# Where ScalarE's first partial-sum copy stands beside a weight cast in three slots of a Strassen projection

## The chip, the cores and the metric

The kernel runs on one core of one Trainium2 chip. The metric is the device time of one execution in microseconds (us). TensorE (PE) multiplies, VectorE (DVE), ScalarE (ACT) and GpSimd (POOL) do the elementwise work, SyncE (SP) issues nearly all loads.

## The reference, cut to what matters

One layer on 512 tokens of width 1024, in float32: an FFN, a mixer, a second FFN, each behind an RMS norm with shift and scale. The two FFNs are the same computation with other weights:

```python
def swiglu(h, w_in, w_out):          # w_in 1024 x 5632, w_out 2816 x 1024
    gu = h @ w_in
    g, u = jnp.split(gu, 2, axis=-1)
    return (jax.nn.silu(g) * u) @ w_out

x = x + HALF_STEP * mod[:, 0, 2][:, None, :] * swiglu(h, ffn1_w_in[l], ffn1_w_out[l])
```

## The kernel before, in words

Each float32 product is made of three passes: an operand is split into a rounded part (`_hi`) and a remainder (`_lo`), and TensorE adds hi x hi, hi x lo and lo x hi. For a weight, ScalarE casts `sw_raw` to `sw_hi` and VectorE subtracts to get `sw_lo_a` or `sw_lo_b`.

The first product of an FFN has 22 tiles of 128 gate and 128 up columns. The first 8 (FFN `f` = 0) or 2 (`f` = 1) are done plainly with 512 moving columns. The other 14 or 20 are Strassen slots `strassen(f, n)`: the tile's product, cut in half three ways, is formed from 7 half-size products ("half-products" 0 to 6) on sums of weight blocks and of activation blocks. A half-product is 12 matmuls of 256 moving columns, so a slot is 84 matmuls. Slots come in two groups, and each is followed by eight down projections (`down2`, 33 matmuls of 512 columns each) that consume 11 tiles of the hidden layer. For `f` = 0 the groups are slots 0 to 2 and 3 to 13, for `f` = 1 they are 0 to 8 and 9 to 19: `N0` = (3, 9) is the first slot of the second group.

The weights of a slot are 7 blocks in three pieces: blocks 0 and 1, blocks 2 to 4, blocks 5 and 6 (1024, 1536 and 1024 columns). Piece 0 and piece 1 are usually cast in the slot before, piece 2 in the slot itself, by `cast_up(f, n, 2)`. In a slot that follows a down projection (n = `N0[f]`) the last block of piece 1 (512 columns) is also cast in the slot, by `cast_up(f, n, 1)`. This block is added up by an accumulating DMA from POOL's queue (line 632), for which the cast waits. In all other slots after the first of an FFN the product of the slot before is finished in between.

Half-products 0, 2 and 4 accumulate in one PSUM region of which intermediate sums are needed. So ScalarE copies that region out after half-product 0 (`keep_sum(f, n, 0)`, 256 columns) before half-product 2 may add to it, half-product 1 after `keep_five` before half-product 3 is started, and so on. Each engine has its own instruction stream, written out by hand in this order; semaphores join them. TensorE's waits in a slot are, in its order: piece 0's remainder, then half-products 0 and 1; then piece 1's remainder (early part) and `q_kept` for the first copy, then half-product 2; then `q_kept` for `keep_five`, then half-product 3; after that half-products 4 to 6, with piece 2's remainder needed by half-product 5.

VectorE's stream in a slot is: remainder of piece 1, second half of the product of the slot before (chained slots), remainder of piece 2, the three weight-block sums of the next slot (`add_blocks`), remainder of its piece 0, then `late_up` and `gates`. SyncE may load the weights of slot n + 2 into a buffer once the remainders of slot n are done, and POOL issues its accumulating DMA once they have landed.

Of the kernel before, what the change touches and what calls it, by code (L numbers as in the profile page):

```python
# [36 lines left out]
def build_program(nc, x, c, w_ada, b_ada, norm_ffn1_g, ffn1_w_in, ffn1_w_out, norm_mix_g, w_mix_in,  # L37
# [62 lines left out]
    N0 = tuple(GF - p for p in PLAIN)  # L100
# [3 lines left out]
    def up_item(f, n):  # L104
        return n + (KD if n >= N0[f] else 0)
# [6 lines left out]
    def pieces(f, i):  # L112
        return sum(3 if j in UP_ITEMS[f] else 1 for j in range(i))
# [4 lines left out]
    def added(f, i):  # L118
        return 16 * sum(1 for j in range(i % 2, i + 1, 2) if j in UP_ITEMS[f])
# [34 lines left out]
    with ctx:  # L154
# [243 lines left out]
        def sw_slot(f, i):  # L398

            return sw_first[:] if f and i == 0 else sw_raw[:, i % 2]  # L400
# [276 lines left out]
        def _(act):  # L677
# [127 lines left out]
            def plain_hi(f, j):  # L805
                act.wait_ge(prod_ready, P_AT[f] + j + 1)
                nc.scalar.copy(b_hi[:, j, :], work[:, 1, :]).then_inc(a_hi_ready, 1)

            def hsum_split(f, r):
                act.wait_ge(hsum_ready[f], HSUMS[r])  # L810
                k0, cols = HSUM_AT[r]
                nc.scalar.activation(sums_hi[:, r], xs[:, k0:k0 + KA, cols], ACT.Copy,
                                     scale=-1.0 if r == 2 else 1.0).then_inc(hsum_hi[f], 1)

            def cast_up(f, n, c):

                i = up_item(f, n)
                if i == 0:
                    act.wait_ge(chunk_done, UP_AT[f] + PLAIN[f] - 1)
                elif i - 1 in UP_ITEMS[f]:  # L820
                    act.wait_ge(sw_used[f], pieces(f, i - 1) + c + 1)
                else:
                    act.wait_ge(sw_used[f], pieces(f, i) - 1 if c == 0 else pieces(f, i))
                act.wait_ge(sw_sum[f], 3 * n + c + 1)
                if c == 1:
                    act.wait_ge(sw_added[f][i % 2], added(f, i))
                j0, j1 = PIECES[c]
                if c == 1 and n == N0[f]:
                    j0 = EARLY[1]
                nc.scalar.copy(sw_hi[:, j0 * BL:j1 * BL], sw_slot(f, i)[:, j0 * BL:j1 * BL])\  # L830
                    .then_inc(sw_hi_ready[f], 1)
# [10 lines left out]
            def cast_down_early(f, g):  # L842

                i = down_item(f, g, 0)
                act.wait_ge(sw_used[f], pieces(f, i) - 2)
                act.wait_ge(sw_full[f][i % 2], landed(f, i))
                nc.scalar.copy(down_hi(0)[:, 0:EARLY_K * P], sw_raw[:, i % 2, 0:EARLY_K * P]).then_inc(early_hi[f], 1)

            def cast_down(f, g, m):

                i = down_item(f, g, m)
                act.wait_ge(sw_used[f], pieces(f, i) - 1 if m == 0 else pieces(f, i - 1))
                act.wait_ge(sw_full[f][i % 2], landed(f, i))
                c = slice(0 if m else EARLY_K * P, DN)
                nc.scalar.copy(down_hi(m)[:, c], sw_raw[:, i % 2, c]).then_inc(sw_hi_ready[f], 1)  # L855

            def keep_sum(f, n, j):

                act.wait_ge(q_done[f], 3 * n + 1 + j)
                if n:  # L860
                    act.wait_ge(gate_ready[f], n)
                nc.scalar.copy(keep[:, j], ps[:, n % 2 * 2, 0:TH]).then_inc(q_kept[f], 1)  # L862

            def keep_five(f, n):
                act.wait_ge(sw_used[f], pieces(f, up_item(f, n)) + 1)
                if n:
                    act.wait_ge(up1_ready[f], n)
                nc.scalar.copy(keep[:, 3], ps[:, n % 2 * 2 + 1, TH:T]).then_inc(q_kept[f], 1)

            def keep_third(f, n):  # L870
                act.wait_ge(sw_used[f], pieces(f, up_item(f, n)) + 2)
                nc.scalar.copy(keep[:, 2], ps[:, n % 2 * 2, 0:TH]).then_inc(q_kept[f], 1)

            def silu_both(f, n):
                act.wait_ge(gate_ready[f], n + 1)
                if n:
                    act.wait_ge(b_prod[f], 2 * n)
                nc.scalar.activation(silu_2, gate, ACT.Silu).then_inc(s_ready[f], 1)

            def product_hi(f, n):  # L880
                act.wait_ge(b_prod[f], 2 * n + 2)
                nc.scalar.copy(b_hi[:, (PLAIN[f] + n) % GF, :], work[:, 1, :]).then_inc(b_hi_ready[f], 1)

            def up_slot(f, n):
                chained = up_item(f, n) and up_item(f, n) - 1 in UP_ITEMS[f]
                second = f == 1 and n == 0
                if n and not chained:
                    cast_up(f, n, 1)
                if n:
                    cast_up(f, n, 2)  # L890
                keep_sum(f, n, 0)
                if chained:
                    product_hi(f, n - 1)
                if f == 0 and n == 0:
                    plain_hi(f, PLAIN[f] - 1)
                keep_five(f, n)
                if second:
                    hsum_split(f, 3)
                keep_sum(f, n, 1)
                if second:  # L900
                    keep_third(f, 0)
                    plain_hi(f, 1)
                if n not in (N0[f] - 1, NS[f] - 1):
                    cast_up(f, n + 1, 0)
                else:
                    cast_down_early(f, 0 if n < N0[f] else 1)
                if not second:
                    keep_third(f, n)
                if n in (N0[f] - 1, NS[f] - 1):
                    cast_down(f, 0 if n < N0[f] else 1, 0)  # L910
                else:
                    cast_up(f, n + 1, 1)
                silu_both(f, n)

            def first_group(f):
                for n in range(N0[f]):
                    up_slot(f, n)
                for m in range(KD):
                    if m < KD - 1:
                        cast_down(f, 0, m + 1)  # L920
                    else:
                        cast_up(f, N0[f], 0)
                        cast_up_early(f)
                    if m == 0:
                        product_hi(f, N0[f] - 1)
# [16 lines left out]
            for n in range(N0[0], NS[0]):  # L942
                up_slot(0, n)
# [87 lines left out]
            for n in range(N0[1], NS[1]):  # L1031
                up_slot(1, n)
# [1137 lines left out]
```

## Time and profile before

| | us |
|---|---|
| median of 3 runs | 857.15 |
| lowest and highest | 853.22 and 858.28 |
| the profiled execution | 860.13 |
| its span in the trace | 858.4 |

The span is what the instruction records cover; 1.73 us of the profiled execution lie outside. The granted TensorE clock is 0.997 of full speed over the span. TensorE is busy for 97% of the span, VectorE 75%, ScalarE 44%, POOL 6%. All times in the rows are from the start of the span of this one execution.

### The profile page before, as it was taken

The numbers are of one execution on the slowest core, as the hardware profiler recorded it, in microseconds if no ns is written. First come the engines' busy times: TensorE is split into PE (matmuls) and PEld (weight loads), VectorE is DVE, ScalarE is ACT, GpSimd is POOL, SyncE is SP. The second block draws the span as 40 slices with busy tenths as digits, with TensorE's granted clock in tenths as the row PEclk, the third lists the DMA queues.
The fourth block names the chain that finished last, engine by engine and source line by source line (L and its number), as shares of the span: only waits on it lengthen the run. The fifth ranks groups of instructions, "written<-read, shape, count | busy, mean of one in ns | idle before, by whom it ended". The sixth has DMA issues, their size and how long they took to land.

```text
span 858.4 us, 14169 instructions
## 1 busy us (share of the span) xinstructions
PE 835.3 (97%) x5767; PEld 746.7 (87%) x5767; DVE 642.7 (75%) x923; ACT 381.2 (44%) x532; POOL 48.4 (6%) x56
## 2 busy tenths in 40 slices
PE   4999999999999999999999999999999999999996
PEld 3778889888999998887887898999988899999886
DVE  4579987877888878858657779988793588885443
ACT  6233346212656652333424256666511366665323
POOL 0000000000000000000430000000000000100000
PEclk9999999999999999999999999999999999999999
DMA  9997566667666666853434802586763567663222
GB/s 282 284 316 250 147 180 207 199 199 191 168 168 166 156 196 180 251 162 100 144 93 118 219 2 74 144 189 172 208 203 106 135 156 176 160 176 107 69 68 98
DMA packets 212733, 142.02 MB, mean 165 GB/s; under 512 B 6216, under 2 KB 191676, under 8 KB 212668
## 3 DMA queue, kind: packets, MB, share of 16 engines
q1 hardware_dynamic: 207716, 132.19, 53.0%
q0 software_dynamic: 4896, 8.92, 6.9%
q8 instruction: 45, 0.74, 0.4%
q14 instruction: 20, 0.16, 0.1%
q10 hardware_dynamic: 56, 0.01, 0.0%
HBM read 130.08 MB, written 2.10 MB: 154 GB/s over the span
## 4 chain that ended last, share of the span: by engine, by line
PE 89%; DVE 4%; SPq 4%; DMA 1%; ACT 1%; issue 1%; ACTq 0%
PE ps L1702 16%; PE ps L1704 16%; PE ps L1703 15%; PE ps L1877 12%; PE ps L1879 12%; PE ps L1881 12%; SPq L485 3%; DMA ada_first<-in_w_ada_dram 1%; PE ps L2003 1%; SPq L447 1%; PE ps L2005 1%; PE ps L2004 1%; DVE h_lo L1114 1%; DVE xs L1107 1%; PE ps L1753 0%
## 5 line engine op out<-in xcount | busy, mean ns | idle before, releaser
L1877 PE MATMUL ps<-sums_hi,sw_hi 128*128 128x256 f32 x544 | 150.9, 277 | 0.6 <-ACT ev L862 0.4
L1879 PE MATMUL ps<-sums_lo,sw_hi 128*128 128x256 f32 x544 | 151.2, 278 | 0.0
L1702 PE MATMUL ps<-b_hi,sw_hi 128*128 128x512 f32 (+1 forms) x374 | 143.7, 384 | 0.0
L1703 PE MATMUL ps<-b_lo,sw_hi 128*128 128x512 f32 (+1 forms) x374 | 140.6, 376 | 0.0
L830 ACT CAST sw_hi<-sw_raw 128x1024 fp32r<-128x1024 f32 (+2 forms) x99 | 116.5, 1181 | 28.6 <-DVE sw_raw L1288 17.8
L1877 PE MATMUL ps<-h_hi,sw_hi 128*128 128x256 f32 x408 | 113.1, 277 | 0.6 <-DVE sw_lo_a L1297 0.6
L1879 PE MATMUL ps<-h_lo,sw_hi 128*128 128x256 f32 x408 | 113.3, 278 | 0.0
L1881 PE MATMUL ps<-sums_hi,sw_lo_a 128*128 128x256 f32 x408 | 112.9, 277 | 0.0
L1877 PEld LDWEIGHTS ps<-sums_hi,sw_hi 128*128 128x128 f32 x544 | 102.1, 188 | 0.9 <-DVE sw_lo_a L1297 0.6
L1879 PEld LDWEIGHTS ps<-sums_lo,sw_hi 128*128 128x128 f32 x544 | 102.0, 187 | 0.0
L1297 DVE TENSOR_TENSOR sw_lo_a<-sw_raw,sw_hi 128x1024 fp32r<-128x1024 f32 x66 | 96.0, 1455 | 5.8 <-ACT sw_hi L830 5.8
L1702 PE MATMUL ps<-h_hi,w_split 128*128 128x512 f32 (+1 forms) x224 | 86.6, 387 | 4.1 <-DVE h_lo L1114 3.9
L1703 PE MATMUL ps<-h_lo,w_split 128*128 128x512 f32 (+1 forms) x224 | 84.4, 377 | 0.0
L1704 PE MATMUL ps<-h_hi,w_split 128*128 128x512 f32 (+1 forms) x224 | 84.3, 376 | 0.0
L1703 PEld LDWEIGHTS ps<-b_lo,sw_hi 128*128 128x128 f32 x374 | 70.3, 188 | 13.5
L1702 PEld LDWEIGHTS ps<-b_hi,sw_hi 128*128 128x128 f32 x374 | 70.3, 188 | 12.3
L1877 PEld LDWEIGHTS ps<-h_hi,sw_hi 128*128 128x128 f32 x408 | 76.6, 188 | 0.9 <-issue 0.7
L1879 PEld LDWEIGHTS ps<-h_lo,sw_hi 128*128 128x128 f32 x408 | 76.5, 187 | 0.2
L1881 PEld LDWEIGHTS ps<-sums_hi,sw_lo_a 128*128 128x128 f32 x408 | 76.6, 188 | 0.0
L1881 PE MATMUL ps<-h_hi,sw_lo_a 128*128 128x256 f32 x272 | 75.3, 277 | 0.0
L855 ACT CAST sw_hi<-sw_raw 128x1408 fp32r<-128x1408 f32 (+1 forms) x32 | 40.3, 1261 | 73.9 <-PE ps L1704 67.4
L1704 PE MATMUL ps<-b_hi,sw_lo_b 128*128 128x512 f32 (+1 forms) x198 | 72.7, 367 | 0.0
(205 smaller groups left out, 1596.8 us busy)
## 6 DMA issues: line engine op xcount, KB each, us to landing
sw_raw<-in_ffn_w_in_dram SPq DMA_DIRECT2D x165, 256.0 KB, 4.4
sw_raw<-in_w_ada_dram SPq DMA_DIRECT2D x16, 1024.0 KB, 5.4
sw_raw<-in_ffn_w_out_dram SPq DMA_DIRECT2D x32, 384.0 KB, 4.4
sw_raw<-in_ffn_w_out_dram SPq DMA_DIRECT2D x32, 320.0 KB, 3.4
w_raw<-in_ffn_w_in_dram SPq DMA_DIRECT2D x19, 512.0 KB, 6.7
sw_raw<-sw_raw POOLq DMA_DIRECT2D x33, 256.0 KB, 3.4
ada_raw<-in_w_ada_dram SPq DMA_DIRECT2D x16, 512.0 KB, 6.0
ada_first<-in_w_ada_dram SPq DMA_DIRECT2D x14, 512.0 KB, 8.2
```

Source lines behind the costliest of these rows:

```text
L447: sp.dma_start(to[:, g, k0:k1], up_w(w)[:, half * KA + k0:half * KA + k1, g, 0:2 * P])\
L485: sp.dma_start(first_w(k)[:, sec], w_ada_v[:, :, col:col + P]).then_inc(first_full[k], 16)
L830: nc.scalar.copy(sw_hi[:, j0 * BL:j1 * BL], sw_slot(f, i)[:, j0 * BL:j1 * BL])\
L855: nc.scalar.copy(down_hi(m)[:, c], sw_raw[:, i % 2, c]).then_inc(sw_hi_ready[f], 1)
L1107: nc.vector.scalar_tensor_tensor(dst, src, gs[:, n, k:k + 1], r, ALU.mult, ALU.mult)\
L1297: nc.vector.tensor_tensor(lo_piece(c)[:, skip:], sw_slot(f, i)[:, j0 * BL + skip:j1 * BL], sw_hi[:, j0 * BL + skip:j1 * BL].bitcast(F32), ...
L1702: nc.tensor.matmul(dst, w_h, a_h, start=start, stop=False)
L1703: nc.tensor.matmul(dst, w_h, a_l, start=False, stop=False)
L1704: return nc.tensor.matmul(dst, w_l, a_h, start=False, stop=stop)
L1877: nc.tensor.matmul(dst, w_h[:, k, :], src_hi[:, k, :], start=start and k == 0, stop=False, skip_group_check=True)
L1879: nc.tensor.matmul(dst, w_h[:, k, :], src_lo[:, k, :], start=False, stop=False, skip_group_check=True)
L1881: ins = nc.tensor.matmul(dst, w_l[:, k, :], src_hi[:, k, :], start=False, stop=stop and k == KA - 1, skip_group_check=True)
```

## The change

In three slots, (f, n) = (0, 3), (1, 9) and (1, 1), the copy after half-product 0 is placed ahead of the cast of piece 2 in ScalarE's stream instead of behind it. No instruction, wait or increment is added or removed.

```diff
             def up_slot(f, n):
                 chained = up_item(f, n) and up_item(f, n) - 1 in UP_ITEMS[f]
                 second = f == 1 and n == 0
+                early_keep = n == N0[f] or (f, n) == (1, 1)
                 if n and not chained:
                     cast_up(f, n, 1)
+                if early_keep:
+                    keep_sum(f, n, 0)
                 if n:
                     cast_up(f, n, 2)
-                keep_sum(f, n, 0)
+                if not early_keep:
+                    keep_sum(f, n, 0)
                 if chained:
                     product_hi(f, n - 1)
```

Slots (0, 3) and (1, 9) open the second group of their FFN; slot (1, 1) is the second slot of its group, and the first with a piece 2 to cast in it.

## Rows read from the trace of the kernel before

**Rows 1.** The page's first part: TensorE's busy time, share and instructions.
```profile
PE 835.3 (97%) x5767; PEld 746.7 (87%) x5767; DVE 642.7 (75%) x923; ACT 381.2 (44%) x532; POOL 48.4 (6%) x56
```
**Rows 2.** From TensorE's waits over the span: total, times, longest (us).
```profile
PE ps L1877 <- ACT ev L862: 0.4, 1, 0.4
```
**Rows 3.** Timeline of TensorE in slot (0, 3): start, duration (us).
```profile
213.02 0.28 PE L1881 MATMUL ps<-sums_hi,sw_lo_a 128*128 128x256 f32 x1
213.43 0.36 PE L1877 MATMUL ps<-sums_hi,sw_hi 128*128 128x256 f32 x1
213.62 0.28 PE L1879 MATMUL ps<-sums_lo,sw_hi 128*128 128x256 f32 x1
```
**Rows 4.** Timeline of ScalarE there; in brackets the idle time before and its releaser.
```profile
211.44 1.58 ACT L830 CAST sw_hi<-sw_raw 128x512 fp32r<-128x512 f32 x2 [4.55 <-DMA sw_raw<-sw_raw]
212.92 0.36 ACT L862 COPY ev<-ps 128x256 f32<-128x256 f32 x1
213.33 0.37 ACT L868 COPY ev<-ps 128x256 f32<-128x256 f32 x1
```
**Rows 5.** Busy time in two windows of 100 us, matmuls into ps alone.
```profile
213.50:313.50 100.00, 100.00 (x844) 1.00 0.63 163
683.00:783.00 100.00, 100.00 (x885) 1.00 0.65 157
```
**Rows 6.** Timeline of TensorE: first matmul of each eleven-slot group, and first behind it.
```profile
210.40 0.28 PE L1877 MATMUL ps<-h_hi,sw_hi 128*128 128x256 f32 x1
...
320.21 0.40 PE L1702 MATMUL ps<-b_hi,sw_hi 128*128 128x512 f32 x1
...
680.60 0.28 PE L1877 MATMUL ps<-h_hi,sw_hi 128*128 128x256 f32 x1
...
785.33 0.39 PE L1702 MATMUL ps<-b_hi,sw_hi 128*128 128x512 f32 x1
```
**Rows 7.** Timeline of VectorE in slot (0, 3).
```profile
213.05 1.23 DVE L1297 TENSOR_TENSOR sw_lo_b<-sw_raw,sw_hi 128x1024 fp32r<-128x1024 f32 x1 [0.26 <-ACT sw_hi L830]
214.19 2.14 DVE L1288 TENSOR_TENSOR sw_raw<-sw_raw 128x512 f32<-128x512 f32 x3
```
**Rows 8.** Timelines in slots (1, 9), (1, 10); last, the page's row of POOL's DMA.
```profile
680.80 1.57 ACT L830 CAST sw_hi<-sw_raw 128x512 fp32r<-128x512 f32 x2 [4.11 <-PE ps L1704]
682.27 0.37 ACT L862 COPY ev<-ps 128x256 f32<-128x256 f32 x1
...
683.33 0.28 PE L1877 MATMUL ps<-sums_hi,sw_hi 128*128 128x256 f32 x1
...
691.01 0.87 POOL L632 DMA_DIRECT2D sw_raw<-sw_raw  x1 [12.77 <-DMA sw_raw<-in_ffn_w_in_dram]
...
697.40 1.49 ACT L830 CAST sw_hi<-sw_raw 128x1536 fp32r<-128x1536 f32 x1
...
sw_raw<-sw_raw POOLq DMA_DIRECT2D x33, 256.0 KB, 3.4
```
**Rows 9.** Timelines of VectorE and ScalarE in slot (1, 1).
```profile
543.67 1.75 DVE L1297 TENSOR_TENSOR sw_lo_a<-sw_raw,sw_hi 128x1536 fp32r<-128x1536 f32 x1
544.33 1.03 ACT L830 CAST sw_hi<-sw_raw 128x1024 fp32r<-128x1024 f32 x1
545.27 0.36 ACT L862 COPY ev<-ps 128x256 f32<-128x256 f32 x1
546.12 0.62 ACT L882 CAST b_hi<-work 128x512 fp32r<-128x512 f32 x1 [0.49 <-DVE work L1345]
546.64 0.37 ACT L868 COPY ev<-ps 128x256 f32<-128x256 f32 x1
```
**Rows 10.** Timeline of TensorE in slot (1, 1), and behind slot (1, 8).
```profile
545.77 0.36 PE L1877 MATMUL ps<-sums_hi,sw_hi 128*128 128x256 f32 x1 [0.45 <-ACT ev L862]
...
547.24 0.28 PE L1877 MATMUL ps<-h_hi,sw_hi 128*128 128x256 f32 x1
...
619.32 0.39 PE L1702 MATMUL ps<-b_hi,sw_hi 128*128 128x512 f32 x1
```

## The prediction

> **What bounds the kernel now.** I read the page's first part, then TensorE's waits, then the timeline of the three slots. TensorE is busy for 97% of the span and no other engine is near that [rows 1], so only time in which TensorE stands still, or runs slower than it could, is to be had. The list of waits puts just one wait down to the copy that the change moves, 0.4 us, once [rows 2]. By that list the change is worth 0.4 us at most. The list is not enough, though: it compares a releaser with the modelled end of the matmul before, and a stop shorter than a matmul's 0.28 us doesn't show in it. So I looked at starts.
>
> In slot (0, 3) the matmuls of half-products 0 and 1 start every 0.113 us (210.40 to 213.02 for 23 steps [rows 3, 6]). The last starts at 213.02, the next not at 213.13 but at 213.43, and the one after 0.19 later [rows 3]. ScalarE ended the copy after half-product 0 at 212.92 + 0.36 = 213.28, and 0.15 later TensorE goes on [rows 3, 4]. In slot (1, 1) the copy ends at 545.27 + 0.36 = 545.63 and TensorE goes on at 545.77, again 0.14 later [rows 9, 10]. So TensorE stood still for the copy in two of the three slots. In (1, 9) the copy was done at 682.64, and half-product 2 began on pace at 683.33 [rows 8]: no wait.
>
> **The pace behind the stop is the larger thing.** From 213.5 on, 844 matmuls start in 100 us, in the same slots of the second FFN 885 [rows 5]: 118.5 against 113.0 ns each, of the same size, with the granted clock at 1.00 in both and about the same DMA traffic (share 0.63 against 0.65). The first 24 matmuls of slot (0, 3) still have the fast pace, the slow one begins with the stop and lasts to the end of the group. The two groups are of eleven equal slots: 320.21 - 210.40 = 109.81 us against 785.33 - 680.60 = 104.73 us [rows 6]. The difference is **5.08 us**, of which the stop itself is 213.43 - 213.02 + 0.19 - 2 x 0.113 = 0.37 us and the pace 4.71 us. The stop in (1, 1), 0.45 + 0.28 - 0.11 = 0.6 us beyond the pace [rows 10], had no such sequel: from 547.24 the 48 + 7 x 84 = 636 matmuls to 619.32 took 113.3 ns each [rows 10]. So a stop can bring the slow pace, and need not; I don't know what decides it.
>
> The Trainium skill, page "TensorE: Matmul & The Clock Gate", Part 1, gives the distance of matmuls at full clock as the columns over 2.4 GHz plus a fixed 2.5 ns or so; for 256 columns that is 109 ns, one figure. The trace has two, 113.0 and 118.5 ns, both above it, at the same granted clock. By that rule only the clock changes the pace, and removing the stop would return 0.37 us and no more; this is the first rival below, whose time is worked out there from rows.
>
> **Part 1, slot (0, 3).** Nothing is added or removed, one copy and one cast change places. The cast of 512 columns started at 211.44, when the accumulating DMA had landed, and with the one of 1024 behind it took 1.58 us in all [rows 4]. The two end at 213.02; the second takes some 1.03 us, as its like in [rows 9], and so the first is over by about 212.0. Half-product 0 ends 12 matmuls before 213.02 + 0.28, at 211.94. The copy can then run from 212.0 to 212.4. Half-product 2 is due at 213.13, and with 0.15 us for the release needs it by 212.98: 0.6 us of slack, so the stop goes. What is late next? Of what half-product 2 waits for, piece 1's early remainder was made before the slot. Half-product 3, due at 213.13 + 1.36 = 214.49, needs `keep_five`; that copy waits for the end of half-product 1 at 213.30 and started at 213.33 [rows 4]. The moved cast now ends at about 213.35 instead of 213.02, so it hardly touches it. Gain: the stop, 0.37 us, and if the slow pace is its consequence, 4.71 us. Upper end 5.08; lower end 0 if another late semaphore takes the copy's place.
>
> Behind the moved cast are queued: piece 2's remainder on VectorE, 213.05 to 214.28 [rows 7], now some 0.35 later, needed by half-product 5 at 213.13 + 3 x 1.36 = 217.2, so 2.6 us of cover; and the three sums of the next slot's blocks, 214.19 to 216.33 [rows 7], now to 216.7, of which the next cast needs the first. Piece 0's remainder is then ready by about 218, and the next slot begins at 219.9: 2 us of cover. SyncE's loads for slot 5 start 0.35 us later. All cost nothing.
>
> **Part 2, slot (1, 9).** No wait to remove, so gain 0. Here the DMA was early and the 512-column cast began at 680.80 with the end of the down projections [rows 8]. ScalarE now stands idle from 681.4 to the end of half-product 0 at 682.15, copies to 682.5, and the piece 2 cast ends at 683.5 instead of 682.37: 1.1 us later. Piece 2's remainder is ready at 684.8, half-product 5 is due at 683.33 + 4.08 = 687.4. The loads of slot 11 start 1.1 us later; POOL's accumulating DMA for them was issued at 691.01 and the cast that needs it started at 697.40 [rows 8]. With 3.4 us to landing [rows 8] it is ready at 695.5 instead of 694.4, 1.9 us of cover. If that cover were gone, the price would be the difference, under 1 us. I take 0.
>
> **Part 3, slot (1, 1).** The copy moves ahead of the 1.03 us cast at 544.33 and ends at 544.7 [rows 9]. But the remainder of piece 1 ends on VectorE at 543.67 + 1.75 = 545.42 [rows 9], and half-product 2 needs it too. TensorE can start at 545.42 + 0.14 = 545.56 instead of 545.77, 0.21 earlier. Half-product 3 began at 547.24, 1.47 behind that, so it would be due at 547.03. It needs `keep_five`, at 546.64 to 547.01, which stands behind the product's cast at 546.12, which waits for VectorE's product and doesn't move [rows 9]. With the release, 547.15: 0.09 us is left of the 0.21, and a restart costs about 0.08 (the 0.19 behind a stop instead of 0.11). Gain 0.0, between -0.1 and +0.2; and this slot now has a stop of 0.4 and a new small one of 0.12 us, where before it had one of 0.6.
>
> **The sum.** Against the profiled execution: 860.13 - 5.08 - 0.0 - 0.0 = 855.05 us. The median of the runs shown lies 2.98 below the profiled execution: 852.07. The three runs lie 5.06 apart, as much as the slow pace costs; I read that, as an estimate, as the slow pace being there in 857.15 and 858.28 and absent in 853.22. The changed kernel should then be at 853.22 less up to 0.4. I take the middle of 852.07 and 852.8, **852.4 us**, its own range 850.5 to 854.2.
>
> **Rivals.**
> 1. The pace isn't the stop's doing (0.26). For: the clock is full, nothing on TensorE's waits shows it, and the stop in (1, 1) had no such sequel. Against: it begins with the matmul behind the stop, and the twin group without a stop never has it. Then 857.15 - 0.4 = 856.7. The same time comes out if the accumulating DMA lands more than 0.6 us later in most executions, so that the stop stays.
> 2. The slow pace goes from the first FFN and comes into the second (0.14), by the stops of Part 3. From half-product 3 to the end of the group are 72.1 us [rows 10]; at 118.5 instead of 113.0 ns they take 0.049 x 72.1 = 3.5 us more: 852.4 + 3.5 = 855.9. For: of the two stops, the shorter (0.30 us) was the one with the slow pace, and the new ones are short. Against: one case is no rule.
> 3. Slower than before (0.08): the same mechanism in slot (1, 1), and no cure in (0, 3), either because rival 1 holds or because the typical run before hadn't the slow pace. 857.15 + 3.5 = 860.6. It decides from the point at which `keep_five` ends later than half-product 3 is due less 0.14 us, which by the above is exceeded by 0.12 us.
> 4. The change does nothing: the copy is bound by the end of half-product 0 or the early cast anyway (0.02), 857.15. The rows speak against it in (0, 3).
>
> **Chances.** The forecast has 0.50. With 852.4 (850.5 to 854.2), 855.9 and 856.7 the range from 850.7 to 857.4 leaves out 860.6, the very ends and little else. One per cent, 8.6 us, is about what a measurement of this kernel can tell from no change; all cases but the tails lie within it: faster by over 1% 0.03, within 0.94, slower by over 1% 0.03.
>
> **What would show it.** In the profile after: matmul starts of slot (0, 3) without a step behind the 24th; the eleven slots from there in 104.7 instead of 109.8 us, 885 matmuls in 100 us; the copy of (0, 3) at 212.0 ahead of the 1024-column cast; in (1, 9) an idle ScalarE before its copy and an unchanged TensorE; in (1, 1) half-product 2 released by the remainder (line 1297) at 0.2 us earlier and half-product 3 by `keep_five`, and 113 ns to the end of that group. I am wrong if the group of (0, 3) has no stop and still 118.5 ns (rival 1), if the group of (1, 1) has 118.5 (rivals 2 and 3), or if the landing of the accumulating DMA moves about by more than 0.6 us.

## The result, and the profile after

| | before | changed |
|---|---|---|
| median of 22 executions each (us) | 854.83 | 857.78 |
| lowest and highest | 853.02, 858.68 | 852.6, 863.46 |
| executions below 855 us | 12 | 3 |
| the profiled execution, its span | 860.13, 858.4 | 856.37, 854.6 |

The ratio is 1.003, 95% interval 1.0017 to 1.0044: a small loss, where a gain of 0.6% was forecast. 857.78 lies 0.38 us above the range. The median of before itself moved with more executions, from 857.15 to 854.83. And the two profiled executions are the other way round, before 860.13, changed 856.37: one execution doesn't tell these kernels apart.

The lines of the page hardly differ. What [rows 1] showed is now:

```profile
PE 835.5 (98%) x5767; PEld 747.2 (87%) x5767; DVE 641.9 (75%) x923; ACT 381.6 (45%) x532; POOL 48.5 (6%) x56
```

The list of TensorE's waits has no row for the copy any more. Its one wait for a weight remainder, 0.6 us, is at the start of slot (1, 1) and stood in the list before too.

**Slot (0, 3)** went as forecast. The timelines of ScalarE and TensorE, answering to [rows 3, 4, 6] (lines are 4 further down than before from here on: 1881 was 1877):

```profile
209.22 0.62 ACT L830 CAST sw_hi<-sw_raw 128x512 fp32r<-128x512 f32 x1 [4.11 <-PE ps L1708]
210.59 0.37 ACT L862 COPY ev<-ps 128x256 f32<-128x256 f32 x1 [0.75 <-PE ps L1885]
210.86 1.06 ACT L830 CAST sw_hi<-sw_raw 128x1024 fp32r<-128x1024 f32 x1
```
```profile
209.02 0.28 PE L1881 MATMUL ps<-h_hi,sw_hi 128*128 128x256 f32 x1
...
211.64 0.28 PE L1885 MATMUL ps<-sums_hi,sw_lo_a 128*128 128x256 f32 x1
211.75 0.28 PE L1881 MATMUL ps<-sums_hi,sw_hi 128*128 128x256 f32 x1
...
313.75 0.39 PE L1706 MATMUL ps<-b_hi,sw_hi 128*128 128x512 f32 x1
```

The copy is over at 210.96, before half-product 2 is due; the step is 0.11 us and the eleven slots take 313.75 - 209.02 = 104.73 us instead of 109.81. But the accumulating DMA was early here: the first cast was released by TensorE and not by the DMA. By the times of [rows 8], where the DMA was early as well, the old order would have kept pace too. The case that the change was made for stands in the profile of e5, one of the experiments below, with the same new order in this slot. There the cast waited for the DMA and began 1.19 us behind the group's first matmul (209.79), against 1.04 us in before, where TensorE stopped. ScalarE and TensorE in e5:

```profile
210.98 0.62 ACT L830 CAST sw_hi<-sw_raw 128x512 fp32r<-128x512 f32 x1 [4.65 <-DMA sw_raw<-sw_raw]
211.51 0.37 ACT L862 COPY ev<-ps 128x256 f32<-128x256 f32 x1
```
```profile
212.41 0.28 PE L1885 MATMUL ps<-sums_hi,sw_lo_a 128*128 128x256 f32 x1
212.52 0.28 PE L1881 MATMUL ps<-sums_hi,sw_hi 128*128 128x256 f32 x1
```

The copy is over at 211.88, and half-product 2 starts on pace at 212.52. The profiles of e6 and e12 show the same, with casts 1.10 and 1.19 us behind the first matmul. So the new order does take this stop away.

**Slot (1, 9)** went as worked out: ScalarE stands idle for 0.75 us before its copy, the cast of piece 2 ends 2.89 us behind the group's first matmul (forecast 2.9, before 1.77), and TensorE has no step in this slot.

**Slot (1, 1)** also went as worked out, to 0.1 us. VectorE, ScalarE and TensorE, answering to [rows 9, 10]:

```profile
536.65 1.75 DVE L1301 TENSOR_TENSOR sw_lo_a<-sw_raw,sw_hi 128x1536 fp32r<-128x1536 f32 x1
```
```profile
537.31 0.35 ACT L862 COPY ev<-ps 128x256 f32<-128x256 f32 x1
537.56 1.05 ACT L830 CAST sw_hi<-sw_raw 128x1024 fp32r<-128x1024 f32 x1
539.10 0.62 ACT L882 CAST b_hi<-work 128x512 fp32r<-128x512 f32 x1 [0.49 <-DVE work L1349]
539.62 0.37 ACT L868 COPY ev<-ps 128x256 f32<-128x256 f32 x1
```
```profile
538.03 0.28 PE L1885 MATMUL ps<-sums_hi,sw_lo_a 128*128 128x256 f32 x1
538.45 0.39 PE L1881 MATMUL ps<-sums_hi,sw_hi 128*128 128x256 f32 x1
538.68 0.28 PE L1883 MATMUL ps<-sums_lo,sw_hi 128*128 128x256 f32 x1
...
539.87 0.28 PE L1885 MATMUL ps<-sums_hi,sw_lo_a 128*128 128x256 f32 x1
540.04 0.38 PE L1881 MATMUL ps<-h_hi,sw_hi 128*128 128x256 f32 x1
```

The copy ends at 537.66, the remainder at 538.40, and TensorE goes on 0.05 behind that (0.14 was forecast): the stop's step from start to start is 0.42 us instead of before's 0.72. The second stop is there too (0.17 from 539.87 to 540.04), made by `keep_five`, which ends at 539.99. In between the matmuls start every 0.119 us, the slow pace; in this execution the fast pace came back with the second stop. From its first matmul to the first one behind it, this group took 612.25 - 525.08 = 87.17 us against 87.21 before, the gain of 0.0 that was forecast.

**The slow pace is now somewhere else.** Windows, TensorE into ps alone: the eleven slots of the first FFN, then slots 9 to 11 and from 12 on of the second ([rows 5] before):

```profile
212.00:312.00 100.00, 100.00 (x885) 1.00 0.69 171
676.00:696.00 20.00, 20.00 (x179) 1.00 0.61 145
707.00:777.00 70.00, 70.00 (x593) 1.00 0.58 150
```

The bracket counts every matmul that touches a window, two or three more than start in it, so 70 us over 593 is a little low. From start to start the trace has 118.6 ns in this stretch and 113.3 ns in the first two. The slow pace begins in slot (1, 12) at a step of 0.15 us, 0.03 too long:

```profile
706.08 0.28 PE L1885 MATMUL ps<-sums_hi,sw_lo_a 128*128 128x256 f32 x1
706.23 0.39 PE L1881 MATMUL ps<-h_hi,sw_hi 128*128 128x256 f32 x1
```
```profile
701.30 1.49 ACT L830 CAST sw_hi<-sw_raw 128x1536 fp32r<-128x1536 f32 x1 [1.34 <-DMA sw_raw<-sw_raw]
...
705.28 0.62 ACT L882 CAST b_hi<-work 128x512 fp32r<-128x512 f32 x1 [0.75 <-DVE work L1349]
705.81 0.37 ACT L868 COPY ev<-ps 128x256 f32<-128x256 f32 x1
```

A cast waited 1.34 us for the accumulating DMA, what ScalarE and VectorE did behind it was late, and `keep_five` ended at 706.18, a hair too late. For 0.03 us of waiting the group took 781.72 - 673.54 = 108.18 us, 3.4 us more than the 104.73 of [rows 6].

### The profile page after: what moved, and what is told of

Same layout as the page of the kernel before. It is cut to its first block, busy times and chain, and to the rows that moved or that the text cites. A ratio compares the mean times of both kernels' runs of the same rounds, so it can differ in the third digit from the quotient of the medians.

```text
span 854.6 us, 14169 instructions
## 1 busy us (share of the span) xinstructions
PE 835.5 (98%) x5767; PEld 747.2 (87%) x5767; DVE 641.9 (75%) x923; ACT 381.6 (45%) x532; POOL 48.5 (6%) x56
## 4 chain that ended last, share of the span: by engine, by line
PE 90%; DVE 4%; SPq 3%; DMA 1%; issue 1%; ACT 1%; ACTq 0%
PE ps L1706 16%; PE ps L1708 16%; PE ps L1707 16%; PE ps L1881 12%; PE ps L1883 12%; PE ps L1885 12%; SPq L485 2%; SPq L447 1%; PE ps L2007 1%; PE ps L2008 1%; PE ps L2009 1%; DMA ada_first<-in_w_ada_dram 1%; DVE h_lo L1118 1%; DVE xs L1111 1%; DVE sw_lo_a L1301 1%
```

## The experiments

Theory S: in slot (1, 1) the changed stop brings the slow pace more often. Theory L: the later cast of piece 2 makes loads and accumulating DMAs late, two and three slots on. Theory N: noise between executions. Ratios have 95% intervals; beside them stands how many executions were below 855 us. That is a count of heaps. The profiles say what the heaps are: with no slow group the execution took 853.7 to 854.0 us (e10, e16, e17), with one it took 856.3 to 857.5 (the changed kernel and e1 to e4, e6 and e7), mostly the second FFN's first group (90.5 instead of 87.2 us in e1 and e3). Which group was slow in an execution without a profile is not known. The granted clock doesn't sort them: over the 35 executions of the kernel before beside e1 to e4 it was 0.9952 on average in those below 855 us and 0.9955 in the others.

**e1 to e3, one slot each** (one chip; before 853.72, 27 of 35 below 855):

```diff
-                early_keep = n == N0[f] or (f, n) == (1, 1)
+                early_keep = (f, n) == (0, 3)        # e1; (1, 9) in e2; (1, 1) in e3
```

> The early copy in slot (0, 3) alone. Theory L (loads): the copy ahead of the cast of piece 2 makes piece 2's remainder up to 1.1 us later, so the weights of the slot after next are loaded later, so the accumulating DMAs and casts two and three slots on are late, and a brief stop of TensorE there brings the slow pace to the end of the group. L expects 1 to 2 us above before in the median, or no change if the removed stop in this slot pays for it, and POOL's DMA for slot 6 at about 22.2 us after the group's start instead of 20.8. Theory S (small stop in slot (1, 1)): nothing of the loss is here, this kernel is at or 0.5 us below before. Theory N (noise between executions): all of the single slots are within 0.1% of before.

Measured: 854.9, ratio 1.0009 (0.9993 to 1.0025), 7 of 12. POOL's DMA for slot 6 was issued 21.5 us after the group's start in the profile, as in e3's with the old order (21.5), and not at 22.2.

> The early copy in slot (1, 9) alone, where no stop was to be removed. L expects most of the loss here: 1.5 to 3 us above before, POOL's DMA for slot 12 at about 22.3 us after the group's start instead of 21.3, its 1536-column cast late. S and N expect no change.

Measured: 853.65, ratio 1.0001 (0.9985 to 1.0018), 8 of 12. POOL's DMA for slot 12 came at 21.2 us, as in before, and not at 22.3. L fails for the median.

> The early copy in slot (1, 1) alone. S expects the loss here: 2 to 3.5 us above before, with 118.5 ns between matmuls in slots (1, 1) to (1, 8). L expects no change within 0.5 us: the group's loads don't hang on this slot's piece 2, whose remainder stands behind the product anyway. N expects no change.

Measured: 856.6, ratio 1.0029 (1.0011 to 1.0047), 2 of 12. S holds here: of the three slots this is the only one whose interval leaves out no change. Its profile has the step of 0.43 us in slot (1, 1), then ten matmuls still at 113.5 ns, then the second stop, a step of 0.23 us. The slow pace begins only behind that one and lasts to the end of the group, 118.6 ns at full clock. Timeline and window of TensorE in e3:

```profile
538.11 0.28 PE L1885 MATMUL ps<-sums_hi,sw_lo_a 128*128 128x256 f32 x1
538.54 0.38 PE L1881 MATMUL ps<-sums_hi,sw_hi 128*128 128x256 f32 x1
...
539.89 0.28 PE L1885 MATMUL ps<-sums_hi,sw_lo_a 128*128 128x256 f32 x1
540.12 0.39 PE L1881 MATMUL ps<-h_hi,sw_hi 128*128 128x256 f32 x1
```
```profile
545.00:605.00 60.00, 60.00 (x509) 1.00 0.66 171
```

**e4, the change with loads ahead** (same chip), and **e10, before with loads ahead** (third chip):

```diff
-                sw_free(f, i)
+                ahead = i >= 2 and i - 2 in UP_ITEMS[f]
+                if ahead:
+                    sp.wait_ge(sw_lo_ready[f], pieces(f, i - 1) - 1)
+                else:
+                    sw_free(f, i)
-                for j, h, side in ((4, 0, 1), (0, 0, 0), (1, 0, 1), (6, 1, 1), (3, 1, 0)):
+                for j, h, side in ((4, 0, 1), (0, 0, 0), (1, 0, 1), (3, 1, 0), (6, 1, 1)):
+                    if ahead and j == 6:
+                        sp.wait_ge(sw_lo_ready[f], pieces(f, i - 1))
```

> All three early copies, and SyncE may load four of the five weight blocks of a slot as soon as the remainders of pieces 0 and 1 of the slot two before are done; only the block of piece 2 still waits for piece 2's remainder. L expects the loss to go, and more: 852.5 to 853.5, with no cast waiting for the accumulating DMA and 113.3 ns throughout. S expects the time of the changed kernel, 3 us above before. N expects no change from before.

Measured: 856.33, ratio 1.0017 (0.9999 to 1.0034), 3 of 12. The interval just takes in no change, but the median is 2.6 us above before's and few executions are below 855: early loads don't take the loss away, again against L. None of the 12 is above 858 us.

> The kernel before with the loads ahead alone. Theory L (late accumulating DMAs make some of the stops): executions above 857.5 us, which need two slow groups or the long one, go; the median falls by 0 to 0.2%, since the stops of slots (1, 0) and (1, 1) stay. If late DMAs play no part: as before.

Measured: 853.58 against 853.96, ratio 0.9993 (0.9974 to 1.0011), 10 of 12, none above 857.4 (before: 5 of 35 above 857.5). Not enough to say that early loads help by themselves.

**e5 to e8** ran on a second chip, where the kernel before had a median of 856.43 and only 8 of 34 executions below 855 (two more, of 928.9 and 2963.92 us, are left out; with them the median is 856.51).

> The change without slot (1, 1): early copies in (0, 3) and (1, 9) alone. Theory S (in slot (1, 1) the changed stop brings the slow pace more often): the loss is gone, within 0.1% of before, most executions near 853 us. Theory L (later loads) is left with little: it would want 0.1 to 0.2% above before.

Measured: 857.18, ratio 1.0007 (0.9983 to 1.0032), 3 of 12.

> The change once more, beside the others on one chip. S: about 0.3% above before, most executions near 856.4 us, 3.3 above the fast ones. Executions above 858 us need a second slow group: L expects some here and none in the kernel that loads ahead.

Measured: 856.54, ratio 1.0000 (0.9977 to 1.0024), 4 of 12. The loss is not there: on this chip the kernel before is as seldom below 855 us as the changed one. e5's profile shows that the old stop in slot (1, 1) brings the slow pace too, behind a step of 0.71 us. It has it a second time in slot (0, 6): a late accumulating DMA makes a step of 0.41 us, the pace stays fast, and it turns slow behind the next step, of 0.23 us.

```diff
+                if (f, n) == (1, 1):
+                    keep_five(f, n)          # e7: ahead of the product's cast, not behind it
                 if chained:
                     product_hi(f, n - 1)
```

> The change, and in slot (1, 1) the copy for half-product 3 ahead of the cast of the product, which waits for VectorE anyway. That takes the second, small stop of the slot away. If the second stop (0.06 us) brings the slow pace, the time falls to that of before or 0.2 below; if the first one does, now 0.31 us long and released by VectorE's remainder, it stays 0.3% above before with 118.5 ns from half-product 2 on.

Measured: 856.38, ratio 0.9991 (0.9970 to 1.0012), 4 of 12. Its profile has no second stop and the slow pace from half-product 2 on: the first stop can be enough, though in e3 it wasn't.

> A version meant to have no stop in any Strassen group: the early copy in (0, 3), and around slots (1, 0) and (1, 1) VectorE's work is put in the order in which TensorE needs it (the first sum of slot (1, 1)'s blocks ahead of the last remainder of the activations, the third sum and the remainder of plain tile 1 behind piece 1's remainder), ScalarE's cast of piece 0 ahead of a copy, its copies ahead of what waits for VectorE. S expects 113.3 ns in all groups in nearly every execution, the two stops of 0.73 and 0.6 us gone, and 851.5 to 852 us with little scatter, 0.2 to 0.4% below before. If the slow pace doesn't come from stops, it is only 0.15% below before and as scattered.

Measured: 856.96, ratio 0.9999 (0.9975 to 1.0022), 3 of 12. Missed. The profile says why: the stops of 0.73 and 0.6 us are gone (the group's first 1.3 us are saved), but in slot (1, 1) `keep_five` was 0.2 us late behind a cast that waited for the third block sum, and in slot (0, 6) there was a step of 0.19 us behind a late accumulating DMA. Behind either the pace is slow.

What e8 changed, on VectorE and ScalarE, beside the early copies of (0, 3) and (1, 1) and e7's edit:

```diff
+            add_blocks(1, 1, 0, 1)               # VectorE: first sum, before hsum_rest(1, 3)
             hsum_rest(1, 3)
...
                 if n:
                     rest_up(f, n, 1)
+                if f == 1 and n == 1:
+                    plain_lo(1, 1)               # was in slot (1, 0), before late_up
+                    add_blocks(1, 1, 2, 3)       # third sum; slot (1, 0) keeps only the second
...
                 if second:
+                    cast_up(f, 1, 0)             # ScalarE: was behind plain_hi
                     keep_third(f, 0)
```

**e9, e11 and e12** (third chip, before 853.96, 22 of 35 below 855). All three have VectorE's third sum one place further ahead; e9 and e11 have the loads ahead, except for slot (1, 3).

```diff
                 if f == 1 and n == 1:            # VectorE, behind piece 1's remainder
-                    plain_lo(1, 1)
                     add_blocks(1, 1, 2, 3)
+                    plain_lo(1, 1)
```

> As the version without stops, with the third sum of slot (1, 1)'s blocks ahead of plain tile 1's remainder (the copy for half-product 3 had ended 0.2 us too late behind it), and with the loads ahead as in the earlier run, so that the accumulating DMA of the fourth slot of a group isn't late. If stops bring the slow pace (theory S): no stop and 113.3 ns in all four groups, 851.5 to 852.3 us in most executions, 0.3 to 0.5% below before. If the slow pace comes by itself: as scattered as before, only the 1.3 us of the two stops lower.

Measured: 854.93, ratio 0.9997 (0.9982 to 1.0013). Ten of 12 stand between 854.5 and 855.3. The profile has two more stops in slot (1, 3), whose loads I had left late, with steps of 0.36 and 0.22 us, and the slow pace behind the second (88.67 us for the group, against 85.69 without a stop in e13).

> The version without stops and with loads ahead, with one stop made on purpose: in slot (1, 10) half-product 2 waits for the copy for half-product 3 as well, which ends some 0.5 us later than half-product 2 is due. S: the stop costs some 0.5 us, and in part of the executions the rest of the group, nine and a half slots, runs at 118.5 ns, 4.2 to 4.4 us more: times in two heaps, near 852.3 and 856.6. If a stop doesn't bring the slow pace: 0.5 us above the version without, in one heap.

Measured: 855.67, ratio 0.9996 (0.9977 to 1.0014), 4 of 12. In the profile the forced step in (1, 10) was 0.83 us and the fast pace went on; the stops in slot (1, 3), which this kernel has from e9's, blur the heaps. Inconclusive.

> The version without stops, but loads as before. S and L together: most executions as the one with loads ahead, some 3 to 5 us above it, where an accumulating DMA was late in the fourth slot of a group. S without L: the same times as with loads ahead.

Measured: 852.22, ratio 0.9976 (0.9957 to 0.9995), 10 of 12 below 855, 9 of them at 851.1 to 853.3. The execution profiled, 854.96, has the stops of slot (1, 3) too (steps of 0.32 and 0.20 us) and the slow pace behind the second.

**e13 to e15: with and without a stop, all else equal** (third chip again, before 854.3, 21 of 35). The load ahead now also covers slot (1, 3) (it waits for the third sum of the slot two before). e14 and e15 add one wait of TensorE to that kernel, before half-product 1:

```diff
+                if (f, n) == (1, 10):
+                    pe.wait_ge(b_prod[f], 2 * n - 1)      # e14; 2 * n in e15
```

> The version without stops with loads ahead also for slot (1, 3), whose weights were late in the last two tries (the step of 0.36 us at 31.2 us after the start of the second FFN's first group); a load ahead now also waits for the third sum of the slot two before. If the slow pace comes only from stops: 113.3 ns in all groups, 851.0 to 851.8 us in nearly all executions, 0.25 to 0.4% below before. If it comes by itself, some executions stay 3 to 5 us above that.

Measured: 852.35, ratio 0.9979 (0.9959 to 0.9998), 9 of 12 at 851.5 to 852.7, three at 855.7 to 858.3. The profile has not one step above 0.12 us in any of the four groups. Whether in the three above 855 us there was a stop, or the slow pace without one, isn't shown.

> The same with one short stop made on purpose in slot (1, 10): half-product 1 waits also for the first half of the product of the slot before, which by the rows of before is released 0.31 us after half-product 1 is due (a step of 0.42 us). If the length decides: most executions have 118.5 ns from there to the end of the group and lie 0.3 + 4.4 = 4.7 us above the stop-free version. If only the place or the releaser mattered in slot (1, 1): 0.3 to 0.4 us above it.

Measured: 857.22, ratio to before 1.0030 (1.0010 to 1.0049), **1 of 12** below 855.

> The same with a longer stop at the same place: half-product 1 waits for the second half of the product, released 0.64 us after it is due (a step of 0.75 us). If the length decides: most executions lie only 0.6 to 0.7 us above the stop-free version, below the kernel with the short stop, though TensorE waits 0.33 us longer. If any stop is as bad as another: as many slow executions as with the short one, and the median 0.3 us above it.

Measured: 857.20, ratio to before 1.0030 (1.0005 to 1.0055), **3 of 12** below 855.

Windows of 80 us in slots 10 to 19 of the second FFN, in e13, then e14, then e15; last, the timeline of the forced stop in e14:

```profile
690.00:770.00 80.00, 80.00 (x708) 1.00 0.59 151
```
```profile
690.00:770.00 80.00, 80.00 (x677) 1.00 0.59 152
```
```profile
690.00:770.00 80.00, 80.00 (x709) 1.00 0.59 151
```
```profile
683.99 0.28 PE L1901 MATMUL ps<-h_hi,sw_lo_a 128*128 128x256 f32 x1
684.33 0.38 PE L1897 MATMUL ps<-sums_hi,sw_hi 128*128 128x256 f32 x1
```

708, 677 and 709 matmuls touch the same 80 us; from start to start they are 113.3, 118.6 and 113.3 ns apart. This is the test of cause: one added wait, all else equal. The stop of e14 is 0.34 - 0.11 = 0.23 us long, and the median rises by 4.9 us: 0.3 for the stop and its restart, the rest from the pace (109.39 instead of 104.73 us for the group in its profile). By the times, a stop of 0.56 us (e15) does the same in most executions, though not in the one profiled. Whether the length decides stays open: 1 of 12 and 3 of 12 can't be told apart.

> The change on this chip. If the length decides: slot (1, 1)'s step of 0.42 us is followed by the slow pace in most executions, wherever before's step of 0.72 us mostly isn't, and the median is about 3 us above that of before; on a chip where the long step brings it as well, both lie near 856.5.

Measured, the change itself beside them: 856.37, ratio 1.0010 (0.9992 to 1.0028), 4 of 12 against before's 21 of 35. The median is 2.1 us higher, the interval takes in no change.

**e17 and e18, again on a fourth chip** (before 853.59, 19 of 23 below 855).

> The early copy in slot (1, 1) alone, again. If its shortened stop brings the slow pace more often than the one of before: at most a third of the executions below 855 us, against half or more of before's, and a median near 856.4. If the first measurement was chance: as before.

Measured: 856.59, ratio 1.0033 (1.0016 to 1.0050), 2 of 12.

> The stop-free version again. Three quarters of the executions or more at 851.5 to 852.7 us, median 0.2 to 0.4% below before, whatever the share of slow executions of before on this chip.

Measured: 851.97, ratio **0.9975** (0.9962 to 0.9988), 12 of 12 at 851.4 to 853.7. It beats the kernel before, and its profile has no stop in any group. On this chip 19 of before's 23 executions are below 855 us, so the gain of 1.6 us is hardly one of pace: the second FFN's first group takes 85.69 us here and 87.2 with before's order at the fast pace (e10's profile), 1.5 us for its two stops and their restarts.

Counted together, without the second chip: kernels with slot (1, 1) as before were below 855 us in 101 of 150 executions of the kernel before and in 25 of 36 of e1, e2 and e10; kernels with the early copy there (the change, e3, e4, e16, e17) in 14 of 70. On the second chip it is 8 of 34 and 3 of 12 (e5) against 8 of 24 (e6, e7), no difference.

## Why the prediction was wrong

**Step by step.** That stops shorter than a matmul don't show in the list of waits, that a stop is followed by a slow pace and that this, not the stop, is what costs: right, and shown by e13 to e15. Its two paces, from counts in windows, were a little low: from start to start they are 113.3 and 118.6 ns. The first rival, which the rule of the Trainium skill's page "TensorE: Matmul & The Clock Gate" (Part 1) would have given, one distance between matmuls at full clock, fell: 113.3 and 118.6 ns both stand at a granted clock of 1.00, in e13 and e14 on either side of a stop of 0.23 us.

**Part 1** held as a mechanism and failed as a term. The step that failed: "The sum. Against the profiled execution: 860.13 - 5.08". The 5.08 us are real in an execution that has them, but the stop needs a late accumulating DMA. Of the five profiles with the old order in slot (0, 3) two have the stop, before and e2, where the first cast began 1.04 and 1.25 us behind the group's first matmul. In e3, e10 and e17 it began 0.2 to 0.4 us behind, and there is none. Of the two, only before has the slow pace behind the stop. I put two of the three times, 857.15 and 858.28, down to the slow pace in this slot, and took that for typical; of 22, twelve were below 855 us. And the profiles of e1, e2 and e5, with the old order in slot (1, 1), have the slow pace behind that slot's stop. That the three times lay as far apart as 5.08 us was chance: a slow group there costs 3.4 us. The term for a median execution is near 0, and e1 measures it: +0.1% (-0.1 to +0.25).

**Part 2** was right about the median: no loss in e2. Its cover was thinner than I had it. The cast of slot (1, 11) did not wait, but in the changed kernel's profile the one of the slot behind waited 1.34 us. Probably the loads of one slot queue behind those of the one before; I had followed the delay for one slot only. Whether the moved cast made this wait or chance did isn't shown: e5's profile has one of 1.80 us in the same place of (0, 3)'s group, e2's none, and e17's, with the old order, has one of 0.48 us there. For the tail theory L isn't out. With both copies early in (0, 3) and (1, 9) and loads as before, 18 of 70 executions are above 858 us (the change, e5, e6, e7, e16), with loads ahead none of 12 (e4); but e3 and e17, without those two copies, have 4 of 24.

**Part 3** had its times right to 0.1 us and its worth wrong. The step that failed: "Gain 0.0, between -0.1 and +0.2", with the slow pace there given 0.14 and 0.08 as rivals 2 and 3. Measured by itself this edit costs 0.29% and 0.33% (e3, e17), 2.5 to 2.8 us, where a slow pace in the eight slots behind it costs 3.4: 80% of the executions with this edit are not below 855 us, against 33% before (without the second chip). Rival 2 named the mechanism and the place, and its 3.5 us fit the 3.35 between e1's and before's group. Its time, 855.9, was too low in part because 852.4 lies 0.7 below the fast heap, and in part, as I read it, for further slow groups, as in the profile's slot (1, 12): 8 of the 22 executions are above 858 us, more than any profile with one slow group in the second FFN has.

**Why the changed stop in (1, 1) is worse than the old one is open.** It is shorter (0.42 instead of 0.72), released by VectorE instead of ScalarE, and followed by a second. e14 and e15 can't tell their two lengths apart, and the second stop isn't needed (e7's profile). In the profiles of the changed kernel, e6, e16 and e17 the fast pace came back after the second stop, so a stop can also end the slow pace. On the second chip old and new are equally bad. What I can say is that each stop is a draw, and the odds differ between stops.

A count over the Strassen groups of all 20 profiles gives a lead. Each stop is sorted by its step from start to start, with the pace that the matmuls took up behind it:

| step of the stop | pace before it | stops | slow behind |
|---|---|---|---|
| 0.84 us, start of (1, 1) | fast | 12 | 0 |
| 0.61 to 0.83 us | fast | 9 | 4 |
| 0.32 to 0.43 us | fast | 14 | 10 |
| 0.15 to 0.23 us | fast | 6 | 6 |
| 0.17 to 0.18 us | slow | 7 | 3 |

The shorter the stop, the more often the slow pace followed. But here length goes together with the place in the slot and with the engine waited for, so this is a count and not a test. It hints at the length, which the times of e14 and e15 leave open.

## What to carry to other kernels

Where the critical engine is full, look at the distance between its starts and not only at its waits: here two equal groups of work differed by 5 us with no wait listed in either. A change that shortens a stop need not gain; the versions with hardly any stop left (e12) or none (e13, e18) did, by 0.21 to 0.25%, most of it the stops' own time. And when executions fall in heaps, one profile shows one heap: take the sum from the heap that is typical, which needs more than three times.

## What the runs showed of the hardware

A series of matmuls with 256 moving columns, each with its own weights, runs at one of two paces from start to start, with the granted clock at 1.00 and equal DMA shares (0.59 in e13 and e14). The fast one is even: nearly always 113 or 114 ns, 113.3 on average. The slow one is uneven: mostly 117 to 119 ns, with 123 to 125 about every ninth time, 118.6 on average (both in before's trace and in all others that have it). The series keeps its pace through hundreds of matmuls (900 in the group of [rows 5]). It changed only at a stop: in the 20 profiles all 80 groups start at the fast pace, and the 56 without a stop keep it to the end. After a stop as short as 0.03 us (the changed kernel's slot (1, 12)) it may go on at the other pace, and after a stop in a slow series it may be fast again (4 of 7). Series of 512 columns showed nothing of this: the down projections behind the first FFN's second group ran at 228.9 ns after a slow group (before) and at 229.7 after a fast one (the changed kernel).
